# Stick-breaking attention layer: order of the copies that empty PSUM banks, and of the projection matmuls beside the attention

## What is computed

```python
def stick_breaking_attention(q, k, v):
    ...
        z = jnp.einsum('bthd,bshd->bhts', q[:, t0:kend], k[:, :kend]).astype(jnp.float32) * scale
        mask = s_idx < t_idx
        log_beta = jax.nn.log_sigmoid(z)
        log_rem = jnp.where(mask, jax.nn.log_sigmoid(-z), 0.0)
        after = lax.cumsum(log_rem, axis=3, reverse=True) - log_rem
        w = jnp.where(mask, jnp.exp(log_beta + after), 0.0)
        outs.append(jnp.einsum('bhts,bshd->bthd', w.astype(v.dtype), v[:, :kend]))
    ...
def mixer_stick_breaking(h, w_in, w_out):
    proj = jnp.einsum('bsd,de->bse', h, w_in)
    q, k, v, g = jnp.split(proj, 4, axis=-1)
    ...
    return jnp.einsum('bse,ed->bsd', o * jax.nn.silu(g), w_out)
...
x = x + mixer_stick_breaking(rmsnorm(x, a_norm[j]), a_w_in[j], a_w_out[j])
return rmsnorm(x, final_norm)
```

## Time and profile before

| | us |
|---|---|
| Median of 3 runs (1623.52 to 1629.39) | 1624.18 |
| Profiled execution, its own time | 1635.98 |
| Its span, first to last instruction | 1634.2 |

### The profile page before, as it was taken

How to read it: one execution, slowest core, us unless ns; L and a number is a source line. 1 busy time by engine, 2 the same in 40 slices (tenths; PEclk the granted TensorE clock), 3 DMA queues, 4 the chain that set the end, 5 groups by cost and what they waited for, 6 DMA issues and landing times. The chain is left out here.

```text
span 1634.2 us, 46030 instructions
## 1 busy us (share of the span) xinstructions
PE 1573.5 (96%) x19314; PEld 1459.2 (89%) x19314; DVE 1282.4 (78%) x1525; ACT 883.9 (54%) x1558; POOL 414.0 (25%) x520
## 2 busy tenths in 40 slices
PE   9999989999999999999999999999999998999998
PEld 7888889899999999998999899999999998868887
DVE  4535338888888888897888898889889897967873
ACT  6635336566655666665655566656655665842221
POOL 0022033224323243323332433324422340000000
PEclk9999989999999999999999999999999999999999
DMA  9968643434334252434343343524253436779621
GB/s 306 274 180 272 183 142 109 124 111 124 124 105 122 88 156 76 140 94 129 105 121 115 111 118 102 152 73 140 81 157 87 123 102 204 249 248 318 203 103 65
DMA packets 205933, 238.57 MB, mean 146 GB/s; under 512 B 54560, under 2 KB 162080, under 8 KB 205728
## 3 DMA queue, kind: packets, MB, share of 16 engines
q1 hardware_dynamic: 113344, 160.30, 32.0%
q10 hardware_dynamic: 92384, 75.33, 15.2%
HBM read 155.78 MB, written 79.76 MB: 144 GB/s over the span
## 5 line engine op out<-in xcount | busy, mean ns | idle before, releaser
L957 PE MATMUL o_ps<-r_turned_hi,dv_head 64*128 64x512 f32 (+3 forms) x1280 | 481.4, 380 | 21.6 <-ACT o_stage L1190 19.7
L1400 DVE TENSOR_TENSOR_SCAN u<-u,u 128x512 f32<-128x512 f32 x384 | 485.5, 1304 | 0.0
L1179 ACT ACTIVATE u<-z_ps 128x512 f32<-128x512 f32 (+3 forms) x640 | 330.9, 533 | 265.1 <-PE z_ps L880 177.0
L923 PE MATMUL group_ps<-hT_hi,w_hi 64*128 64x256 f32 x1888 | 453.6, 281 | 2.9 <-DVE made L1384 2.0
L957 PE MATMUL o_ps<-r_turned_lo,dv_head 64*128 64x512 f32 (+3 forms) x1280 | 454.1, 365 | 0.0
L923 PE MATMUL group_ps<-hT_hi,w_lo 64*128 64x256 f32 x1888 | 448.8, 280 | 0.0
L923 PE MATMUL group_ps<-hT_lo,w_hi 64*128 64x256 f32 x1888 | 447.6, 279 | 0.0
L1404 DVE TENSOR_TENSOR r_turned_lo<-turn_ps,r_turned_hi 128x1024 fp32r<-128x1024 f32 (+1 forms) x320 | 337.5, 1055 | 130.6 <-ACT r_turned_hi L1184 129.8
L1184 ACT ACTIVATE r_turned_hi<-turn_ps 128x1024 fp32r<-128x1024 f32 (+1 forms) x320 | 287.5, 899 | 172.6 <-PE turn_ps L902 149.6
L923 PEld LDWEIGHTS group_ps<-hT_hi,w_hi 64*128 64x128 f32 x1888 | 318.5, 186 | 8.1 <-DVE made L1384 2.8
L923 PEld LDWEIGHTS group_ps<-hT_lo,w_hi 64*128 64x128 f32 x1888 | 314.4, 186 | 2.1
(11 more groups left out here) (180 smaller groups left out, 3253.2 us busy)
## 6 DMA issues: line engine op xcount, KB each, us to landing
qk_hi_cols<-made ACTq DMA_DIRECT2D x128, 128.0 KB, 2.4
qk_lo_cols<-made ACTq DMA_DIRECT2D x128, 128.0 KB, 2.5
k_hi_twice<-qk_hi_cols SPq DMA_DIRECT2D x128, 128.0 KB, 3.2
k_lo_twice<-qk_lo_cols SPq DMA_DIRECT2D x128, 128.0 KB, 3.6
x_T<-in_xT SPq DMA_DIRECT2D x29, 512.0 KB, 6.5
w_raw<-in_w_qkg SPq DMA_DIRECT2D x24, 512.0 KB, 4.0
x_rows<-in_x SPq DMA_DIRECT2D x16, 512.0 KB, 4.8
v_rows<-v_stage ACTq DMA_DIRECT2D x32, 256.0 KB
```

The costliest lines, as they stand in the source:

```text
L923: last = nc.tensor.matmul(bank_of(g)[:, 0:GW], a[t % 2][rows, k, :], b[rows, c // 2, k, cols], start=(n == 0 and not low), stop=(n == QPM ...
L957: last = nc.tensor.matmul(o_ps[:, 0:w], dv_head[rows, j * CB + sigma_block(m), :], turned_part[p % 2][rows, here], start=first, stop=(end ...
L1179: nc.scalar.activation(u_t[(m // CB) % RU][r][:, 0:w], score_bank(m), ACT.Sigmoid, scale=-Z_SCALE).then_inc(s_u, 1)
L1400: nc.vector.tensor_tensor_scan(u, u, other, start, ALU.mult, op).then_inc(s_r, 1)
```

## The change

Four edits:

1. ACT: `made_high` and `store_high` stand behind `hi` of the turn, where they stood ahead of it. DVE: `made_low` stands behind `lo`. Only if the bank is needed within the first half of this turn's lower-row matmuls (`needed_soon`) does the old place stay.
2. ACT: `empty` stands between the turn's two sigmoids, where it stood behind both. `store_low` stands behind both, where it stood ahead of them.
3. PE: `left` lets the upper rows come no closer than 26 matmuls to the lower rows at any point, where so far only their count at the end of a turn was bound.
4. `y_banks`: the four pairs rotate from block 0 on, and the waits of blocks 1, 3 and 4 follow.

```diff
--- before.py
+++ after.py
@@ -171,6 +171,14 @@
 for g in range(FIRST, NG):
     at = (g - FIRST + 1) * QPM + BEHIND
     FINISHED.setdefault(min(h for h in range(2 * NU) if UPTO[h + 1] >= at), []).append(g)
+
+
+def needed_soon(g, h):
+
+    again = (g + 3 - FIRST) * QPM - UPTO[h]
+    return again < (UPTO[h + 1] - UPTO[h]) // 2
+
+
 DONE = [-LEAD_SCORES - 1] * BEFORE + [CB * s + CB - 1 for s in sorted(AHEAD) for _ in AHEAD[s]]
 DONE += [PAIR * h + 1 for h in sorted(FINISHED) for _ in FINISHED[h]]
 LOAD_W = {DONE[FINAL_G[t - 2]] + 1: t for t in range(2, NT)}
@@ -455,7 +463,7 @@
 
         def y_banks(n):
 
-            return y_ps[max(n - 1, 0) % len(y_ps)]
+            return y_ps[n % len(y_ps)]
 
         last_banks = y_banks(LAST) + [y_banks(LAST - 3)[0]]
 
@@ -928,6 +936,8 @@
                 def left(h, low):
 
                     limit = UPTO[h + 1] - BEHIND if low else UPTO[h + 1]
+                    if low and made_so_far[0] < STREAM:
+                        limit = min(limit, made_so_far[0] - QPM - 2)
                     return max(0, min(limit, STREAM) - made_so_far[low])
 
                 def group_pairs(h, share):
@@ -1003,11 +1013,9 @@
                             pe.wait_ge(s_plow, 2 * PIECES)
                         if t >= 2 and i % OUTM == 0:
                             pe.wait_ge(s_mlo, t - 1)
-                        if m == 0 and n == 1:
-                            pe.wait_ge(s_res, f + 1)
-                        if m == 0 and n == len(y_ps):
+                        if m == 0 and n == len(y_ps) - 1:
                             pe.wait_ge(s_ost, H * NC)
-                        if m == 0 and n >= len(y_ps) + 1:
+                        if m == 0 and n >= len(y_ps):
                             pe.wait_ge(s_res, 2 * (n - len(y_ps)) + f + 1)
                         a, b = ((m_hi, wo_hi), (m_hi, wo_lo), (m_lo, wo_hi))[m % 3]
                         tok = slice(n % GB * P, (n % GB + 1) * P)
@@ -1284,23 +1292,29 @@
                     ended = chunk_end(s - 1) if inside(s - 1) else None
                     for part in range(2):
                         h, first = 2 * s + part, CB * s + PAIR * part
-                        for g in finished(h - 1):
+                        soon = [g for g in finished(h - 1) if needed_soon(g, h)]
+                        for g in soon:
                             made_high(g)
                             store_high(g)
                         if inside(s):
                             hi(h)
                         for g in finished(h - 1):
-                            store_low(g)
+                            if g not in soon:
+                                made_high(g)
+                                store_high(g)
                         if inside(s + LEAD):
                             stick(first + LEAD_SCORES)
+                        if ended is not None and part == 0:
+                            empty(ended)
+                        if inside(s + LEAD):
                             stick(first + LEAD_SCORES + 1)
+                        for g in finished(h - 1):
+                            store_low(g)
                         if s - 1 in AHEAD:
                             store_low(AHEAD[s - 1][part])
                         if s in AHEAD:
                             made_high(AHEAD[s][part])
                             store_high(AHEAD[s][part])
-                        if ended is not None and part == 0:
-                            empty(ended)
                         if ended is not None and part == 1:
                             store_o(ended)
                         for m in range(first, first + PAIR):
@@ -1518,10 +1532,14 @@
                 for s in range(-LEAD, LAST_SLOT + 1):
                     for part in range(2):
                         h, first = 2 * s + part, CB * s + PAIR * part
-                        for g in finished(h - 1):
+                        soon = [g for g in finished(h - 1) if needed_soon(g, h)]
+                        for g in soon:
                             made_low(g)
                         if inside(s):
                             lo(h)
+                        for g in finished(h - 1):
+                            if g not in soon:
+                                made_low(g)
                         for m in range(first + LEAD_SCORES - PAIR, first + LEAD_SCORES):
                             if 0 <= m < NS:
                                 scan(m)
```

## The result

| | us |
|---|---|
| Changed kernel, median of 4 runs (1726.07 to 1728.44) | 1727.05 |
| Kernel before, same chip, median of 4 (1623.52 to 1633.39) | 1626.79 |
| Ratio | 1.0611 [1.0573, 1.0650] |
| Span of the profiled executions, before and after | 1634.2 and 1726.7 |

The change makes the kernel 100 us slower, where the prediction had +18 and a range up to 1666.

What follows compares the result with a forecast made beforehand. The prediction took PE, with both row halves filled, to bound a full-width attention turn, DVE close behind. Its terms -25 + 7 - 18 + 54 = +18 us on the median 1624.2 gave 1642, range 1604 to 1666.

Steps and rivals of the forecast that it cites:

- What bounds the kernel: Attention, full-width turn: bound by PE with both row halves filled, 3.95 us needed against 3.94 seen.
- Edit 3, +54: PE, end of a turn: six lower-row then six upper-row matmuls leave one half idle; +54 us, ends 36 and 74.
- The rule of three: PE: an operation is handed to its half in written order, only while at most three of that half wait.
- priced at half for every dry start: PE: a half that ran dry restarts 0.1 us late; half of that gives 54 us in all.
- the walk's upper end (74): Both written orders walked over turns 4 to 310, full 0.1 us restart at each dry start: 74 us longer.
- Edits 1 and 2, -43: PE's waits shrink: -25 us at transposes by earlier turned copies, -18 us at products by earlier copy of o_ps.
- the signs that were to show the forecast right: Among them, PE's waits for the turned low part below 5 us and for o_stage below 6.
- the waits only move: Rival: transposes wait because DVE is late, half of the 43 stays; +39, 1663; chance 0.20 together with full restart.
- Late banks, +7: PE projections: `made_low` ends later, so banks come free later; 10 us lost, 2.0 us of old waits go.
- Edit 4, 0: Output stage: no bank wait is shown, so none is removed; nothing gained or lost.
- the rival in which the restart counts in full and the waits go: Every dry start pays the full restart: 74 + 7 - 43 = +38; chance 0.20 together with waits only moving.

Runs made afterwards that it cites:

- e3: Changed kernel with the cap on the upper rows only in the first part of a turn; measured 1651.85 us, ratio 1.0148.
- e1: Changed kernel without edit 3, so edits 1, 2 and 4 stay; measured 1635.77 us, ratio 1.0049.
- the cap alone: Kernel before with edit 3 alone, the bound on the upper rows; measured 1729.88 us, ratio 1.0629.
- e6: Kernel before with edit 1 alone, low stores also moved behind the sigmoids; measured 1657.38 us, ratio 1.0171.
- e5: Kernel before with edit 2 alone, o_ps copied between the sigmoids and low stores behind both; measured 1618.23 us, ratio 0.9933.

## Why the prediction was wrong

The direction was right (slower), and so was the place: edit 3, on PE, in the attention. The size was off by a factor of more than five.

- **What bounds the kernel**: right. A full turn of 3.95 us is filled on both halves, and what breaks the pairing adds time.
- **Edit 3, +54, the step that failed.** It measured about 136 us: 75 for the long runs at the end (changed kernel against e3) and 61 for the short middle (e3 against e1, waits counted). The rule of three was right: in none of these traces does one half run further ahead. The end is not six and six throughout, as the prediction says, but up to twelve and ten. The restart was priced at half for every dry start, because I saw one without it. In the changed kernel it depends on how long the half stood. Among projection matmuls the second one is late (0.19 or more behind the first) in all 198 places where the half had stood over 0.2 us past its usual beat of 0.12, and in 10% of the 347 where it had stood 0.1 to 0.2. The 75 lie by the walk's upper end (74), but that walk was for all of edit 3, so the agreement is no proof. The 61 are a wait in the code (`s_wu`, `s_wl`) that has hardly a row in the profile of before (0.2 us, once), because 0.7 us of matmuls or more always covered it. I costed the moved matmuls by where they went, and not what they had covered where they stood.
- **Edits 1 and 2, -43.** PE's waits did fall, from 49 to 8 us, and those for the low part (2.9) and for o_stage (3.5) met the signs that were to show the forecast right. But the longer turns did that; the cap alone does it too. Edit 2 alone is worth 11, not 18, with 7.1 us of waits for the earlier store left. Edit 1 alone loses 28 us. Its gain at the transposes is about 6 (22.7 to 16.2), not 25. The group's copy is out of the way: of the 13.7 us (23 waits) that stood behind it before, 0.9 are left. But in its place the turned copy comes late behind ACT's other work, store issues and the copies of weights and of v's differences. The rival "the waits only move" had the number (half stays) but not the cause: it put the rest on DVE, and in e6 DVE stood idle ahead of the low part in 21 of the 25 waits (14.4 of the 16.2 us).
- **Late banks, +7.** In the changed kernel 0, since the longer turns cover them. Without the cap 22.8 us: I had priced them in the new PE order alone, where the banks are asked for about a microsecond later. In turn 62 of e1 the low part ends 3.60 us behind the transposes' start, where I had 3.45.
- **Edit 4, 0**: right.
- **The sum.** 136 for edit 3, less some 56 of waits (41 listed, and 0.16 for each of the 95 that are gone), is 80; 100 were measured. Some 20 us are not placed. Four are waits that went between e3 and the changed kernel and that the 75 leaves out. The other 15 or so lie already between the kernel before and e1: e1 waited 48.0 us in 69 waits against 48.9 in 106, so by the same count it should have been 7 us faster, and it was 8 slower. Both end their turns with alternating matmuls, so the length of runs is not the cause; it stays open. One part is that a listed wait is not always worth 0.16 more: in e5 49 waits for o_stage with 12.6 us went, for a gain of 11.
- **The range.** Its upper end came from the rival in which the restart counts in full and the waits go. The wait that I did not know was in no case. The direction came out right by edit 3 alone: without it the forecast was a gain of 36, and e1 measured a loss of 8.

## What to carry to other kernels

Before you move work away from a place, list every wait that the code has right behind that place, the ones with no row, or hardly one, in the profile first: a wait that is always covered is priced by the work that covers it. When two row halves of TensorE work side by side, alternate them, or keep runs at three or less. And if PE is the bound, short waits of PE after a change prove nothing for the edits on the other engines, since a slower PE shortens them by itself.

## What the runs showed of the hardware

- One row half goes on only while at most three operations of the other half wait, in both directions: upper behind lower (424.90 with 424.89) and lower behind upper (425.37, 425.48, 425.60). Runs of three cost 8 us and runs of four 25 over alternating ones in 300 turns; the changed kernel's runs of up to twelve cost 75.
- A half that stood for long restarts with 0.1 us extra at its second matmul (0.22 for 0.12 at 425.12, 0.34 for 0.23 at 427.62): always where it had stood over 0.2 us past its beat (198 of 198 places), seldom at 0.1 to 0.2 (10% of 347).
- A matmul that waits for another on PE itself starts at the earliest 0.10 us behind the recorded end of that one, in none of 280 turns sooner, and what is written behind it stands too (the scores at 427.28). With 512 columns the recorded end is 0.39 us behind the start. The view of waits lists this wait once in the whole attention.
